# Prompt attention from transposed scores, with another split of the convolution's taps, in a one-step hybrid decoder

## What is computed

```python
s = einsum('nqhd,nkhd->nhqk', q, k) * ATTN_SCALE      # 512 x 512 per head
s = s + f_q[..., :, None] - f_k[..., None, :]         # cumulated log forget values
s = where(k_pos <= q_pos, s, -inf)
p = softmax(s, axis=-1)
out = einsum('nhqk,nkhd->nqhd', p, v)
```

## Time and profile before

| | us |
|---|---|
| median of 3 runs (1321.18 to 1323.65) | 1321.43 |
| the profiled execution | 1322.46 |
| its span on the core | 1320.7 |
| PE busy in the span | 1269.7 |
| DVE busy | 626.7 |
| ACT busy | 459.6 |
| POOL busy | 167.1 |

### The profile page before, as it was taken

One profiled execution on the slowest core, in us unless ns is written; L12 is line 12 of the kernel. 1 busy time (PEld: TensorE's weight loads), 2 busy tenths in 40 slices (PEclk: granted clock), 3 DMA queues, 4 the chain that ended last, 5 costly groups with the idle time before them and its releaser, 6 DMA issues.

```text
span 1320.7 us, 22854 instructions
## 1 busy us (share of the span) xinstructions
PE 1269.7 (96%) x9658; PEld 1207.7 (91%) x9658; DVE 626.7 (47%) x860; ACT 459.6 (35%) x725; POOL 167.1 (13%) x181
## 2 busy tenths in 40 slices
PE   6998898889999999999999999989999999999998
PEld 5998794456999999999999999989999999999998
DVE  5587797744353334243334444664533433432431
ACT  5624435444343123132133333533331321321321
POOL 3055830100210000000000222032000000000000
PEclk9999998799999999999999999999999999999999
DMA  5331130231242222222222222212223223212211
GB/s 152 99 110 36 51 128 34 96 112 34 96 129 82 79 96 97 77 83 95 96 77 84 96 89 72 96 37 77 84 97 96 69 92 96 95 65 94 97 65 68
DMA packets 111755, 113.17 MB, mean 86 GB/s; under 512 B 6414, under 2 KB 105882, under 8 KB 111663
## 3 DMA queue, kind: packets, MB, share of 16 engines
q1 hardware_dynamic: 110111, 107.50, 25.3%
q0 software_dynamic: 1472, 4.44, 1.1%
q10 hardware_dynamic: 88, 0.02, 0.0%
HBM read 107.21 MB, written 5.16 MB: 85 GB/s over the span
## 4 chain that ended last, share of the span: by engine, by line
PE 85%; DVE 5%; POOL 5%; ACT 2%; issue 1%; DMA 1%; SPq 0%; ACTq 0%; POOLq 0%; DVEq 0%
PE ps L656 75%; PE ps L825 2%; POOL nat_buf L559 2%; PE ps L847 2%; POOL nat_buf L566 1%; DVE c_f L1506 1%; PE ps L912 1%; DMA w_raw<-in_w_in_ab 1%; PE ps L802 1%; PE ps L886 1%; PE ps L838 1%; DVE prob L1603 1%; POOL nat_buf L564 1%; PE ps L940 1%; POOL A_lo L631 1%
## 5 line engine op out<-in xcount | busy, mean ns | idle before, releaser
L656 PE MATMUL ps<-A_hi,w_hi 128*128 128x272 f32 x1408 | 294.5, 290 | 7.8 <-DVE xT L1456 4.2
L656 PE MATMUL ps<-A_lo,w_hi 128*128 128x272 f32 x1408 | 292.6, 289 | 0.0
L656 PE MATMUL ps<-A_hi,w_lo 128*128 128x272 f32 x1408 | 291.6, 289 | 0.0
L1095 ACT ACTIVATE w_hi<-w_raw 128x1024 fp32r<-128x1024 f32 x180 | 188.9, 1050 | 264.3 <-DVE xT L1717 249.3
L656 PE MATMUL ps<-B_hi,w_hi 128*128 128x272 f32 x1280 | 265.9, 289 | 0.0
L656 PE MATMUL ps<-B_lo,w_hi 128*128 128x272 f32 x1280 | 264.9, 288 | 0.0
L656 PE MATMUL ps<-B_hi,w_lo 128*128 128x272 f32 x1280 | 263.9, 288 | 0.0
L656 PEld LDWEIGHTS ps<-A_hi,w_hi 128*128 128x128 f32 x1408 | 222.8, 190 | 10.2 <-ACT xT L1125 4.6
L656 PEld LDWEIGHTS ps<-A_hi,w_lo 128*128 128x128 f32 x1408 | 222.7, 190 | 0.0
L1430 DVE TENSOR_TENSOR w_lo<-w_raw,w_hi 128x1024 fp32r<-128x1024 f32 x180 | 219.8, 1221 | 6.0 <-ACT w_hi L1095 6.0
L656 PEld LDWEIGHTS ps<-A_lo,w_hi 128*128 128x128 f32 x1408 | 221.1, 190 | 0.0
(11 more groups left out here) (273 smaller groups left out, 1081.1 us busy)
## 6 DMA issues: line engine op xcount, KB each, us to landing
w_raw<-in_w_ff_up SPq DMA_DIRECT2D x64, 512.0 KB, 4.4
w_raw<-in_w_ff_down SPq DMA_DIRECT2D x64, 512.0 KB, 4.2
w_raw<-in_w_in_ab SPq DMA_DIRECT2D x20, 512.0 KB, 4.7
w_raw<-in_w_in_c SPq DMA_DIRECT2D x16, 512.0 KB, 3.9
w_raw<-in_w_out_ab SPq DMA_DIRECT2D x8, 512.0 KB, 4.5
k_pg<-in_cache_k SPq DMA_DIRECT2D x16, 256.0 KB, 3.6
v_pg<-in_cache_v SPq DMA_DIRECT2D x16, 256.0 KB, 3.7
w_raw<-in_w_out_c SPq DMA_DIRECT2D x8, 512.0 KB, 3.9
```

Source lines behind the costliest of these rows:

```text
L656: mm = pe.matmul(ps[:, 2 * s + half, 0:HALF], wt[:, j % 4, k, :], mv[:, k, half * HALF:(half + 1) * HALF], start=(k == 0 and at_ == 0), st ...
L1095: act.activation(w_hi[:, j % 4], w_raw[:, b % 2, :, P * (j % 2):P * (j % 2) + P], ACT.Copy)\
```

## The change

The softmax's maximum is still found from queries x keys scores, block q = 3 first. Then the scores are computed a second time, transposed (keys x queries), with the negative maximum added by a matmul: `spread_max` writes a 128 x 512 tile with the maxima on diagonals, and `ones_r` (fp32r) times it adds each query's maximum to its column. ACT takes the exponent straight from PSUM into `pT`, with no bias and no sum. `values` takes `pT` as the stationary operand, 128 x 128, and 128 moving columns: 64 of values and 64 of ones, so that the row sum comes out beside the result; `normalise` divides 64 columns per block. The result is queries x dims and is turned once per pair of heads (`turn_pair`, 4 transposes). Loops run over head and block, with PE one head ahead in `scores`; values are two heads behind. The division of the probabilities, the 80 transposes and the 32 copies are gone.

```diff
-CONV_GLU, CONV_QK, CONV_V = [4, 4, 2, 0], 3, 3
-CONV_ATT = [2] * 5 + [1] * 17 + [0] * 10
+CONV_GLU, CONV_QK, CONV_V = [4, 4, 5, 4], (3, 2), 3
+CONV_ATT = [2, 2, 1, 1] * 5 + [0] * 20
-LN_MEAN, LN_VAR = 22, 29
+LN_MEAN, LN_VAR = 24, 31
...
-                        sp.wait_ge(s_done, QT * (2 * j + 2))
+                        sp.wait_ge(st_done, QT * (2 * j + 2))
...
+            link(pool.memset(ones_r[:, :].bitcast(F32), 1.0))
+            link(pool.memset(v_all[:, TT * H * HD:], 1.0))
             pool.memset(f_aug[:, :, :, :], 1.0).then_inc(consts, 1)
...
+            def scores(h, i):
+                s, q = QT * h + i, QT - 1 - i
                 if s == 0:
                     pe.wait_ge(aug_evac, 4 * TT)
+                if s < 2:
+                    pe.wait_ge(nat_evac, 6 * TT - 1 + s)
+                if s >= 2:
+                    pe.wait_ge(max_done, s - 1)
...
+            def scores_T(h, j):
+                s = QT * h + j
+                if j == 0:
+                    pe.wait_ge(diag_ok, h + 1)
+                if s >= 2:
+                    pe.wait_ge(exp_done, s - 1)
+                n, out = S - P * j, ps[:, 2 + s % 2, :]
+                pe.matmul(out[:, 0:n], kT[0:HD + 2, h, NS + P * j:NS + P * j + P], qT[0:HD + 2, h, NS + P * j:T],
+                          start=True, stop=False, skip_group_check=True)
+                pe.matmul(out[:, 0:P], mask_b[:, :], ident_b[:, :], start=False, stop=False, skip_group_check=True)
+                pe.matmul(out[:, 0:n], ones_r[:, :], neg_max[:, h % 2, :, :].rearrange("p q c -> p (q c)")[:, P * j:S],
+                          start=False, stop=True, skip_group_check=True).then_inc(st_done, 1)
...
-                if m == 6 * TT - 3:
-                    scores(0)
...
+                pe.wait_ge(exp_done, QT * (h + 1))
+                if h == 0:
+                    pe.wait_ge(aug_evac, 4 * TT)
+                else:
+                    pe.wait_ge(norm_done, h)
+                for q in range(QT):
+                    for j in range(q + 1):
+                        c0 = S * j + P * (q - j)
+                        mm = pe.matmul(ps[:, 4, P * q:P * q + P], pT[h % 2][:, c0:c0 + P], value_window(j, h),
+                                       start=(j == 0), stop=(j == q), skip_group_check=True)
                 mm.then_inc(pv_done, 1)
...
+            for s in range(QT * (H + 2)):
+                h, i = s // QT, s % QT
+                if h < H:
+                    scores(h, i)
+                if i == 0 and h >= 2:
+                    values(h - 2)
+                if 1 <= h <= H:
+                    scores_T(h - 1, i)
+                if i == QT - 1 and h >= 2 and h % 2 == 1:
+                    turn_pair((h - 2) // 2)
...
+                act.activation(pT[h % 2][:, S * j:S * j + n], ps[:, 2 + s % 2, 0:n], ACT.Exp).then_inc(exp_done, 1)
...
-                conv(CONV_QK if m < 4 * TT else CONV_V if m < 6 * TT - 1 else 0)
+                conv(CONV_QK[m % 2] if m < 4 * TT else CONV_V if m < 6 * TT - 1 else 0)
...
+            def spread_max(h):
+                dve.wait_ge(max_done, QT * (h + 1))
+                if h >= 2:
+                    dve.wait_ge(st_done, QT * (h - 1))
+                dve.tensor_tensor(neg_max[:, h % 2, :, :],
+                                  ident[:, :].rearrange("p (a c) -> p a c", a=1).broadcast_to([P, QT, P]),
+                                  soft[:, 3 + h % 2, :].rearrange("p (q a) -> p q a", a=1).broadcast_to([P, QT, P]),
+                                  ALU.mult).then_inc(diag_ok, 1)
...
+                link(dve.reciprocal(ri[:, :].rearrange("p (q a) -> p q a", a=1), out[:, :, HD:HD + 1]))
+                dve.tensor_tensor(att_nat[:, :, HD * (h % 2):HD * (h % 2) + HD], out[:, :, 0:HD],
+                                  ri[:, :].rearrange("p (q a) -> p q a", a=1).broadcast_to([P, QT, HD]), ALU.mult)\
+                   .then_inc(norm_done, 1)
...
+            for s in range(QT * (H + 2)):
+                h, i = s // QT, s % QT
+                if h < H:
+                    maximum(h, i)
+                    if i == QT - 1:
+                        spread_max(h)
+                if i == 1 and h >= 2:
+                    normalise(h - 2)
+                if i == 2 and h >= 4 and h % 2 == 0:
+                    pair_lo((h - 4) // 2)
                 if s == 5:
                     forget_rows()
-                conv(CONV_ATT[s])
+                if s < len(CONV_ATT):
+                    conv(CONV_ATT[s])
```

More of the change, by code:

```diff
@@ L829, in _, with turn_pair @@
                     turn_heads(m - 2)
-                if m == 6 * TT - 3:
-                    scores(0)
[L833 to L839, removed]
-            def values(h):
[L842 to L850, removed]
-                mm.then_inc(pv_done, 1)
+            def values(h):
+                pe.wait_ge(exp_done, QT * (h + 1))
[8 more added lines that the diff above has]
+                                       start=(j == 0), stop=(j == q), skip_group_check=True)
+                mm.then_inc(pv_done, 1)
+            def turn_pair(p2):
+                pe.wait_ge(norm_done, 2 * p2 + 2)
+                if p2:
+                    pe.wait_ge(ml_done, p2)
+                for q in range(QT):
+                    mm = pe.transpose(ps[:, 5, P * q:P * q + P], att_nat[:, q, :], ident[:, :])
+                mm.then_inc(oT_done, 1)
             def column_sums(src, ready, count, done):
@@ L1194, in _, with exponent @@
             mx, rs = soft[:, 0, :], soft[:, 1, :]
[L1196 to L1202, removed]
+            def exponent(h, j):
+                s, n = QT * h + j, S - P * j
+                if s == 0:
+                    act.wait_ge(glu_stored, 16 * (NB + 1))
+                if s == QT:
+                    act.wait_ge(psum_red, CT)
+                if j == 0 and h >= 2:
+                    act.wait_ge(pv_done, h - 1)
+                act.wait_ge(st_done, s + 1)
+                act.activation(pT[h % 2][:, S * j:S * j + n], ps[:, 2 + s % 2, 0:n], ACT.Exp).then_inc(exp_done, 1)
             act.wait_ge(glu_done, CT)
             for m in range(6 * TT):
-                if m == 6 * TT - 1:
-                    exponent(0)
                 nat_step(m)
@@ new lines, in normalise @@
+            def normalise(h):
+                dve.wait_ge(pv_done, h + 1)
+                if h == 0:
+                    for s in range(3):
+                        dve.wait_ge(k_stored[s], 16 * len([m for m in range(2 * TT, 4 * TT) if m % 3 == s]))
+                if h >= 2 and h % 2 == 0:
+                    dve.wait_ge(oT_done, h // 2)
+                out = ps[:, 4, :].rearrange("p (q c) -> p q c", q=QT)
+                link(dve.reciprocal(ri[:, :].rearrange("p (q a) -> p q a", a=1), out[:, :, HD:HD + 1]))
+                dve.tensor_tensor(att_nat[:, :, HD * (h % 2):HD * (h % 2) + HD], out[:, :, 0:HD],
+                                  ri[:, :].rearrange("p (q a) -> p q a", a=1).broadcast_to([P, QT, HD]), ALU.mult)\
+                   .then_inc(norm_done, 1)
@@ L1628, in centre @@
                                          in1=two(c_f[:, c, :]), op0=ALU.mult, op1=ALU.add).then_inc(cx_done, 1)
-            for s in range(H * QT):
-                maximum(s)
-                if s != 1:
-                    share(max(s - 1, 0))
-                if s % (2 * QT) == 3 and s > 2 * QT:
-                    pair_lo(s // (2 * QT) - 1)
+            for s in range(QT * (H + 2)):
+                h, i = s // QT, s % QT
+                if h < H:
[6 more added lines that the diff above has]
+                    pair_lo((h - 4) // 2)
                 if s == 5:
                     forget_rows()
-                conv(CONV_ATT[s])
+                if s < len(CONV_ATT):
+                    conv(CONV_ATT[s])
                 if s in SPLIT_ATT:
@@ L1645, in _ @@
             assert next_step[0] >= V_STEPS
-            share(H * QT - 1)
             pair_lo(PAIRS - 1)
```

81 lines of the change are left out of this document (27 added, 54 removed).

## The result

| | before | after |
|---|---|---|
| median of 4 runs each, us | 1321.73 | 1331.41 (1329.75 to 1331.99) |
| profiled execution, us | 1322.46 | 1331.0 |
| its span, us | 1320.7 | 1329.3 |

The account below looks back on a forecast made before the run. Attention was taken as bound by hand-overs and DVE at first, then by a slow PE after each lull. -4.7 + 2.5 + 1.5 + 4.85 - 5.3 - 0.3 = -1.45, giving 1320.0 us against the medians; range 1314.5 to 1326.

Parts of the forecast that it names:

- After 320 us PE is busy for 992 of 1001 us at the full clock; nothing of that is touched.: Program after 320 us: PE busy at the full clock and untouched by the change, so no term in the sum.
- The clock, +2.5: Attention fill: one clock fall; a 7 us stretch costs 2.2 (half, less DVE's cost in head 1), 10 us costs 4.1.
- the clock holds: Rival, attention fill: no fall of the clock, so 2.5 goes: 1317.5 us, down to 1315; chance 0.3.
- The stage at the full clock, -4.7 and +1.5: Attention: 73.85 us summed step by step against 78.5, plus 1.5 (0 to 2.7) for what the hand sum leaves out.
- the bound 0.107: Attention's `values`: lower bound per matmul pass, which the columns alone need, against 0.117 taken and 0.135 as upper bound.
- The taps in the fill: Attention fill: taps 2, 2, 1 on DVE between maxima and spread, 3.3 us of the 6.9 us fill.
- Taps in GLU and QK, -0.45: Projections: seven more taps in the GLU stage cost +4.85, ten fewer in the QK stage give -5.3; bounds +2 to -2.
- the prediction's estimate from the exclusive lock: QK stage: each tap that goes is worth 0.66 if ports lock for a whole instruction, 6.6 in all.
- V projection, -0.3: V projection: `scores(0)` leaves it, 0.3 us less.
- Waits costed at nothing: SP's value pages wait for `st_done`, about a head later; all read after the attention: nothing, or 8 us if waited for.
- The second rival: Attention, between heads: the clock falls again and again, three stretches, 24 us at 1.2 GHz: +6.7, 1328; chance 0.15.
- the first rival: Attention fill: the clock holds, 2.5 goes, 1317.5 us, and 1315 if the 1.5 goes as well; chance 0.3.

Follow-up runs that it names:

- a_pad58: Kernel after with 58 instructions of already satisfied waits ahead of PE's first transpose: 1324.33 us, ratio 1.0026.
- a_busy: Kernel after with 29 matmuls of constants, never read, in PE's waits of the fill and first transposed scores, moving its program by 58 instructions: 1320.28 us.
- a_fill0: Kernel after, moved by 58 instructions, with the attention's 30 taps begun only after the first head: 1317.85 us, ratio 0.9973.
- b_taps: Kernel before with the change's new lists of taps alone, PE's program unchanged: 1325.17 us, ratio 1.0036.
- b_fill0: Kernel before with its 27 attention taps begun only after the first head: 1324.74 us, ratio 1.0028.
- a_pad120: Kernel after moved by 120 instructions of satisfied waits, 58 at the start and 62 in the attention's fill: 1338.56 us, ratio 1.0133.
- b_pad58: Kernel before with 58 instructions of already satisfied waits ahead of PE's first transpose: 1328.45 us, ratio 1.0055.
- a_best1: Kernel after, moved by 58, old projection tap lists, 27 attention taps begun after the first head, column sums later, pair copy earlier: 1312.89 us, ratio 0.9942.
- a_order: Kernel after, moved by 58 instructions, with last column sums three steps later and ACT's pair copy ahead of a head's first exponent: 1324.14 us, ratio 1.0026.
- a_best2: As a_best1, with its 27 attention taps spread thinner over steps 4 to 24 and column sums at steps 27 and 36: 1311.41 us, ratio 0.9921.

## Why the prediction was wrong, point by point

* **"After 320 us PE is busy for 992 of 1001 us at the full clock; nothing of that is touched."** This sentence failed, and it carries nearly two thirds of the miss (7.1 of 11.4 us, by the medians of after and a_pad58). The change left that program as it was but moved it in PE's list, and the loop's jump back then cost 3.9 us in the first pass (468.3 to 568.4 takes 100.1 us against 96.2) and 4.0 in the second, which starts with a further stop and runs at 0.50 until 575: the 7.9 us above. The sum had no term for it and the range none either; without it (a_pad58) the kernel stands at 1324.33, inside the range, though still slower than before.
* **The clock, +2.5.** One fall in the fill and none after came as forecast; the length of the slow stretch did not. I let it end after 7 to 10 us, like those of the old stage; it lasted 17 and cost at least 4.8 (a_busy) and up to 7.0 (against a_fill0). The rule by which I priced it, half the stretch less 1.3 under DVE, gives 7.2 for 17 us, so the price of a microsecond was not the step that failed. Why the stretch lasted so long stays open: PE has work all through (7.00 of 7 and 8.00 of 8 us), but so it had in the old stage from 212 to 218 (6.00 of 6). The rival "the clock holds" came true, for the fill, only where PE was kept busy or DVE freed: the clock fell after a fill in which PE was busy for 3.83 of 6 us, and did not fall when the same waits were filled with matmuls.
* **The stage at the full clock, -4.7 and +1.5.** Right: 75.35 us forecast, 76.8 in a_busy, whose 12 matmuls of constants behind the first transposed scores are 2.5 us of PE; 81.6 less 7.0 is 74.6. The fill was 7.1 (6.9 forecast), passes of `values` are 0.114 apart (I took 0.117; the row of L907 had it, and the bound 0.107 is out), loop heads 8.2 to 8.5 apart, 9.0 with a column sum (8 to 8.3 forecast), and from the start of the last `values` to the sampled part it is 3.7 us (4.35 forecast with the wait ahead of them). The taps in the fill were counted at 3.3 us and taken as given; a_fill0 shows that they need not be paid.
* **Taps in GLU and QK, -0.45.** The first term was about right (+4.85; 4.9 measured in b_taps, 5.3 in after), the second too large: -5.3 forecast, -4.1 and -4.2 measured, so together +0.8 and +1.1, inside the bounds. POOL's third operation gained 3.0 us in all (1062 to 909 ns on the mean of 20), not the 4.0 that 0.5 in eight steps make, and its first 0.6, not the 1.3 of two whole taps. By the prediction's estimate from the exclusive lock of the Trainium skill (SBUF — State Buffer, SBUF: two separate sides) it would be 6.6; the measurement is further from that than from mine.
* **V projection, -0.3**: `scores(0)` left it, and the first four scores now stand behind it in the fill, where they were counted. It was not measured by itself.
* **Waits costed at nothing**: the sampled part took 39.5 us against 39.4 with its pages fetched later. Right.
* **The second rival** gave 1328 with the right sign for the wrong reason: several falls between heads. The trace shows one stretch at 0.50 in the attention.

In sum, against the profile before: -1.45 forecast; +1.1 + 3.3 + 0.1 + 6.4, less 2.3 of start, came. Three sums of the prediction are a little off as they stand, and none changes this account: the parts of the fill add up to 6.8 and not 6.9, a slow stretch of 10 us costs 3.7 by the rule given and not 4.1, and the first rival with the 1.5 gone as well is 1316 and not 1315.

## What to carry to other kernels

An edit ahead of a long hardware loop also moves the loop in its engine's instruction list: look at the loop's jump back in the trace ("issue" before it, packets of the instruction queue in its second pass) before a difference is put down to the edit, and compare at a shift that is free of the stop. When work moves to an engine that becomes the bound, price its slow clock for as long as it may last (17 us here, where 7 to 10 were taken from the old stage), and take other engines' filler work out of the stretch in which it waits. A list that suits one schedule (taps in the fill) need not suit the next: here the kernel with the new attention was 9 us faster than before, and only with another list. What the old attention could win with a list made for it was tried with one list alone (b_fill0).

## What was not expected of the hardware

* The jump back of a loop of 768 matmuls costs 7 to 9 us or nothing (the rest took 1007.1, 1007.8 and 1008.6 us with the stop, 999.2 to 1000.8 without), by its place in the list to within 58 instructions: three stops in the ten loops of the five kernels above, with 74 or 75 packets of 16 KB on q8 in the kernels that have one, and 64 or 66 in those that do not.
* A wait that is already satisfied is not free on PE: 62 instructions of two waits each held it for up to 6.1 us (a_pad120), and with the 58 at the start PE's first matmul came at 8.7 us in place of 5.3 (a_pad58 and b_pad58, after and before).
* The clock fell for about 3.4 us near 880 us in some of the profiles (before, a_fill0, a_busy, a_best1) and not in others with the same program there (a_pad58, a_order, a_best2); the rest took 1000.7 to 1000.8 us with it and 999.2 to 999.3 without. Where such a fall comes in one profile only, 1.5 us of a difference are not the edit's.
